# Neighbourhood attention on 64-row products: one query split for all heads in place of zero-padded buffers

## The chip, the cores and the metric

One Trainium2 chip, of which the kernel uses one core. The metric is the device time of one execution in microseconds (us); less is better. All engines of the core run side by side and wait for each other on semaphores.

## The reference

Two transformer blocks follow one another on 512 tokens of width 1024. The change lies in the second one (two layers, `l` = 0 and 1), in its neighbourhood attention. Each of 4 heads of width 64 has 512 queries; layer 0 also has 256 context queries, which attend to the context alone:

```python
s_loc = einsum('brqhd,brikhd->bhrqik', qg, k_band) * scale + bias   # 8 grid rows of 64 keys
s_loc = where(in_win, s_loc, -inf)
s_ctx = einsum('brqhd,blhd->bhrql', qg, k_ctx) * scale              # 256 context keys
p = softmax(concatenate([s_loc, s_ctx], -1))
o = einsum(p_loc, v_band) + einsum(p_ctx, v_ctx)
# context queries, layer 0 only
yc_b = dense_attention(q_ctx, k_ctx, v_ctx)
```

Everything is float32. The contraction of a score is over the 64 channels of one head.

## The kernel before

All work is written out by hand for each engine's queue, with semaphores between them; nothing is reordered by a scheduler. Most of the time goes to weight products ("units", function `gemm`): a float32 operand is split into a high part, rounded to the TensorE's fp32r format, and a low part (the rest), and `product` (lines 592 to 595) makes three matmuls: hi by hi, lo by hi, hi by lo. L593, L594 and L595 are the lines of all such matmuls, of the units and of the scores of neighbourhood attention alike.

After the projections of a layer come two attentions, one after the other: differential attention ("diff", lines 1633 for its exponentials and 2296 to 2307 for maximum and mix) and neighbourhood attention ("na"). Both go through `attention`, which works on items: one head and one tile of 128 queries. Layer 0 has 24 items (16 of 768 keys, then 8 context items of 256 keys), layer 1 has 16. For item i TensorE does, in this order:

1. the scores of item i + 2 (`na_score`), into one of two PSUM areas, once the exponential of item i has been taken;
2. the value products of item i - 1 (L989), once ScalarE has copied its transposed probabilities (`pt`, L1623);
3. the transposes of the probabilities of item i (L1001).

VectorE adds the bias (L2359), takes the maximum (L2362), scales a finished head (L2321), and in between squares the diff output (L2335, L2337). ScalarE takes the exponential (L1663) and makes the copy L1623. At item 6 both split the first unit of the output projection (ScalarE L1209, VectorE L1820).

Two heads share the 128 partitions of a query or key tile: head h has rows 64 (h % 2) to 64 (h % 2) + 63 of chunk h // 2. The kernel before still contracts over all 128 rows. For that it keeps zero-padded queries, `qz_hi[parity]` and `qz_lo[parity]`: tiles whose other 64 rows are zero. VectorE clears the four of them before diff attention of each layer (L2340), and for each head in turn ScalarE fills the 64 rows of the high part (`nqz_his`, L1639) and VectorE those of the low part (`nqz_los`, L2375): the first head near the end of diff attention, the next three at the beginning of na, the context heads as their turn comes. The keys (`nak`, `nakc`) are split once, for all heads (ScalarE L1647, L1652; VectorE L2379, L2382).

```python
q_hi, q_lo = (z[it.head % 2][:, c, tok] for z in (qz_hi, qz_lo))
if not it.ctx:
    product(dst[:, 0:S], q_hi, q_lo, nak_hi[:, c, :], nak_lo[:, c, :], True, True)
a_ = 0 if it.ctx else S
product(dst[:, a_:a_ + SC], q_hi, q_lo, nakc_hi[:, c, :], nakc_lo[:, c, :], True, True).then_inc(na_s, 1)
```

Of the kernel before, what the change touches and what calls it, by code (L numbers as in the profile page):

```python
# [17 lines left out]
F32 = mybir.dt.float32  # L18
F32R = mybir.dt.float32r
ALU = mybir.AluOpType  # L20
# [3 lines left out]
P = 128  # L24
DM = 1024
KT = DM // P
S = 512
SC = 256
# [15 lines left out]
HD = 64  # L44
# [95 lines left out]
def build(nc, d, out):  # L140
# [16 lines left out]
    with ctx:  # L157
        def at(name, shape, dtype, offset):

            return nc.alloc_sbuf_tensor_at(name, shape, dtype, offset=offset)  # L160
# [44 lines left out]
        H0 = o  # L205
# [106 lines left out]

        qz_hi = [at(f"qz_hi{i}", [P, 2, S], F32R, H0 + 4096 * i) for i in range(2)]
        qz_lo = [at(f"qz_lo{i}", [P, 2, S], F32R, H0 + 8192 + 4096 * i) for i in range(2)]
        nak_hi = at("nak_hi", [P, 2, S], F32R, Q2 + 8192)
        nakc_hi = at("nakc_hi", [P, 2, SC], F32R, Q2 + 20480)
# [25 lines left out]
        def result_bank(par, j):  # L342
# [49 lines left out]
        (df_s, df_split, df_mx, df_e1, df_e2, df_comb, df_t, df_pt, df_pv, df_out, ss_ready, ystd_ready, yd_ready, df_hi,  # L392
         nqz_ready, qz_zero, nqzhi_done, nk_hi, nk_split) = (
            sem(n_) for n_ in ("df_s1", "df_split", "df_max", "df_e1", "df_e2", "df_comb", "df_t", "df_pt", "df_pv", "df_out",
                               "df_squares", "df_std", "df_normed", "df_hi", "nqz_ready", "qz_zero",
                               "nqz_hi_done", "nk_hi", "nk_split"))
        na_s, na_mx, na_exp, na_t, na_pt, na_pv, na_out = (
# [193 lines left out]
        def _(pe):  # L591
            def product(dst, lhi, llo, rhi, rlo, start, stop):
                pe.matmul(dst, lhi, rhi, start=start, stop=False)  # L593
                pe.matmul(dst, llo, rhi, start=False, stop=False)  # L594
                return pe.matmul(dst, lhi, rlo, start=False, stop=stop)  # L595
# [408 lines left out]
            for l in range(2):  # L1004
# [119 lines left out]
                def na_score(i, it):  # L1124
                    c = it.head // 2
                    tok = slice(it.tile * P, (it.tile + 1) * P)
                    dst = S3[i % 2]
                    if it.pos == 0:
                        pe.wait_ge(nqz_ready, g0 + it.group + 1)
                    if i < 2:  # L1130
                        pe.wait_ge(df_e2, i0 + len(its) - 1 + i)
                    else:
                        pe.wait_ge(na_exp, i0 + i - 1)
                    q_hi, q_lo = (z[it.head % 2][:, c, tok] for z in (qz_hi, qz_lo))
                    if not it.ctx:
                        product(dst[:, 0:S], q_hi, q_lo, nak_hi[:, c, :], nak_lo[:, c, :], True, True)
                    a_ = 0 if it.ctx else S
                    product(dst[:, a_:a_ + SC], q_hi, q_lo, nakc_hi[:, c, :], nakc_lo[:, c, :], True, True).then_inc(na_s, 1)

# [59 lines left out]
        def _(act):  # L1199
# [364 lines left out]
            for l in range(2):  # L1564
# [71 lines left out]

                def nqz_his(it):
                    r_ = slice(HD * (it.head % 2), HD * (it.head % 2 + 1))
                    act.copy(qz_hi[it.head % 2][r_, it.head // 2, 0:SC if it.ctx else S],  # L1639
                             (naqc if it.ctx else naq)[r_, it.head // 2, :]).then_inc(nqzhi_done, 1)  # L1640

                df_exps(0, its[0])
                for i in range(N_):
                    if i + 1 < N_:
                        df_exps(i + 1, its[i + 1])
                    if i == N_ - 4:
                        act.copy(nak_hi[:], nak[:]).then_inc(nk_hi, 1)  # L1647
                    elif i == N_ - 3:
                        act.wait_ge(qz_zero, 4 * (l + 1))
                        nqz_his(first_of[0])  # L1650
                    elif i == N_ - 2:
                        act.copy(nakc_hi[:], nakc[:]).then_inc(nk_hi, 1)  # L1652
                    take_pt(i, its[i], df_t, df_pt, df_pv)
                for it in first_of[1:4]:
                    nqz_his(it)

                def na_exps(i, it):
# [9 lines left out]
                for i in range(N_):  # L1667
                    if i + 1 < N_:
                        na_exps(i + 1, its[i + 1])
                    if its[i].pos == its[i].size - 1 and its[i].group + 4 < len(first_of):  # L1670

                        nqz_his(first_of[its[i].group + 4])
                    take_pt(i, its[i], na_t, na_pt, na_pv)
                    if i == 6:
                        hi(n + 9)
# [42 lines left out]
        def _(dve):  # L1718
# [487 lines left out]
            for l in range(2):  # L2206
# [131 lines left out]

                for z in (*qz_hi, *qz_lo):
                    dve.memset(z[:].bitcast(F32), 0.0).then_inc(qz_zero, 1)  # L2340
                df_max(0, its[0])
# [27 lines left out]

                def nqz_los(it):  # L2370

                    dve.wait_ge(nqzhi_done, g0 + it.group + 1)
                    r_ = slice(HD * (it.head % 2), HD * (it.head % 2 + 1))
                    w_ = SC if it.ctx else S
                    dve.tensor_tensor(qz_lo[it.head % 2][r_, it.head // 2, 0:w_], (naqc if it.ctx else naq)[r_, it.head // 2, :],  # L2375
                                      qz_hi[it.head % 2][r_, it.head // 2, 0:w_].bitcast(F32), ALU.subtract).then_inc(nqz_ready, 1)

                dve.wait_ge(nk_hi, 2 * l + 1)
                dve.tensor_tensor(nak_lo[:], nak[:], nak_hi[:].bitcast(F32), ALU.subtract).then_inc(nk_split, 1)  # L2379
                nqz_los(first_of[0])  # L2380
                dve.wait_ge(nk_hi, 2 * l + 2)
# [7 lines left out]
                for i in range(N_):  # L2389
                    if i < 3:  # L2390
                        nqz_los(first_of[i + 1])
                    if 3 <= i < 3 + len(first_of):
                        last = df_squares(first_of[i - 3])
                        if i - 3 == len(first_of) - 1:
                            last.then_inc(ss_ready, 1)
                            dve.tensor_tensor(yv, yv, bc(subln[:], 4 * T), ALU.mult)
                    if i and its[i - 1].pos == its[i - 1].size - 1:
                        na_take(its[i - 1])
                    if i + 2 < N_:

                        if its[i + 2].pos == 0 and not its[i + 2].ctx:
                            mask_bias(its[i + 2].head)
                        dve.wait_ge(na_exp, i0 + i + 1)
                        na_max(i + 2, its[i + 2])
                    if its[i].pos == its[i].size - 1 and its[i].group + 4 < len(first_of):
                        nqz_los(first_of[its[i].group + 4])
                    if i == 6:
                        lo(n + 9, (n + 9) % 2)
# [179 lines left out]
```

## Time and profile before

| | |
|---|---|
| runs shown | 3055.95, 3068.29, 3068.49 us, median 3068.29 |
| profiled execution | 3062.02 us, its span 3060.4 us |
| TensorE busy | 2931.8 us (96%), weight loads 2503.1 us (82%) |
| VectorE, ScalarE busy | 1688.0 us (55%), 988.0 us (32%) |
| na attention | 1605.7 to about 1680 us (layer 0), 2574.4 to about 2632 us (layer 1) |

The span is the time between the first and the last instruction of the profiled execution; 1.6 us lie around it. PE is TensorE's matmul, PEld its weight load, which runs beside matmuls; DVE is VectorE, ACT ScalarE, SP the engine that issues most DMAs. A row of the trace names the line, the engine, the operation and its tiles. "[0.53 <-X]" at its end says for how long the engine had been idle before it and what ended that.

### The profile page before, as it was taken

To read this page: it belongs to the slowest core of one execution; us is meant where nothing else is said; L and a number is where in the kernel's file an instruction comes from. 1 tells how busy PE (TensorE), PEld (TensorE's weight loads), DVE (VectorE), ACT (ScalarE), POOL (GpSimd) and SP (SyncE) were. 2 spreads that over 40 slices of the span, in tenths; PEclk is the share of its full clock that TensorE was granted. 3 is DMA by queue.
4 is the path that set the end of the run, shared out by engine and by line. 5 is a ranking of instruction groups with operands and counts; after the bars stand their busy time and mean duration, and the time that the engine had idled before them with its cause. 6 is when DMAs were issued, how large, how long until landed. Compare 5 with 4: busy or idle time off the path is not lost.

```text
span 3060.4 us, 39832 instructions
## 1 busy us (share of the span) xinstructions
PE 2931.8 (96%) x15873; PEld 2503.1 (82%) x15873; DVE 1688.0 (55%) x2280; ACT 988.0 (32%) x1367; POOL 106.5 (3%) x150
## 2 busy tenths in 40 slices
PE   6999999999999999999888999999999988899999
PEld 5888787979788888789777888888888967788887
DVE  5656655454556676464486555455555248554444
ACT  3333333232333222322265232122223226433222
POOL 0000000000001100000000000000000000000000
PEclk8999999999999999999979999999999999999999
DMA  6333344535234544233430213223322142122332
GB/s 236 115 123 114 113 152 139 173 111 164 73 117 124 180 147 131 97 100 97 110 84 15 83 35 96 85 84 91 101 76 83 56 114 53 56 74 86 103 105 73
DMA packets 269999, 319.00 MB, mean 104 GB/s; under 512 B 25323, under 2 KB 236667, under 8 KB 269852
## 3 DMA queue, kind: packets, MB, share of 16 engines
q1 hardware_dynamic: 243676, 232.83, 24.8%
q0 software_dynamic: 19456, 72.00, 7.7%
q10 hardware_dynamic: 6720, 12.06, 1.2%
q8 instruction: 110, 1.80, 0.3%
q14 instruction: 37, 0.30, 0.0%
HBM read 294.05 MB, written 11.27 MB: 100 GB/s over the span
## 4 chain that ended last, share of the span: by engine, by line
PE 83%; DVE 6%; ACT 3%; DVEq 2%; SPq 2%; issue 1%; DMA 1%; ACTq 0%
PE psum L593 24%; PE psum L594 24%; PE psum L595 24%; PE psum L989 2%; SPq L549 2%; PE psum L759 1%; PE psum L805 1%; PE psum L1001 1%; DVE n_t L1808 1%; DVE w_lo L1820 1%; DVE dneg L2296 1%; DMA ada<-in_w_ada 1%; PE psum L873 1%; DVEq L1807 1%; DVE sba L2307 1%
## 5 line engine op out<-in xcount | busy, mean ns | idle before, releaser
L1820 DVE TENSOR_TENSOR w_lo<-raw,w_hi 128x2048 fp32r<-128x2048 f32 (+1 forms) x244 | 435.3, 1784 | 421.7 <-ACT w_hi L1209 311.5
L593 PE MATMUL psum<-hs_hi,w_hi 128*128 128x512 f32 x1632 | 648.8, 398 | 14.8 <-DVE hs_lo L1812 5.7
L595 PE MATMUL psum<-hs_lo,w_hi 128*128 128x512 f32 x1632 | 638.8, 391 | 0.0
L594 PE MATMUL psum<-hs_hi,w_lo 128*128 128x512 f32 x1632 | 638.7, 391 | 0.0
L593 PEld LDWEIGHTS psum<-hs_hi,w_hi 128*128 128x128 f32 x1632 | 308.2, 189 | 89.5 <-issue 13.3
L595 PEld LDWEIGHTS psum<-hs_lo,w_hi 128*128 128x128 f32 x1632 | 308.2, 189 | 65.7
L594 PEld LDWEIGHTS psum<-hs_hi,w_lo 128*128 128x128 f32 x1632 | 308.7, 189 | 62.7 <-issue 1.2
L1874 DVE SCALAR_TENSOR_TENSOR ada_acc<-ada_raw,csil,ada_acc 128x512 f32<-128x512 f32 x392 | 279.7, 749 | 45.1 <-DMA ada_raw<-in_w_ada 25.7
L593 PE MATMUL psum<-mid_hi,w_hi 128*128 128x512 f32 x768 | 300.5, 391 | 0.0
L594 PE MATMUL psum<-mid_hi,w_lo 128*128 128x512 f32 x768 | 299.7, 390 | 0.0
L595 PE MATMUL psum<-mid_lo,w_hi 128*128 128x512 f32 x768 | 299.3, 390 | 0.0
L1217 ACT CAST w_hi<-raw 128x2048 fp32r<-128x2048 f32 (+1 forms) x138 | 191.4, 1387 | 325.6 <-PE psum L595 293.3
L2128 DVE SCALAR_TENSOR_TENSOR r_t<-psum,r_t 128x512 f32<-128x512 f32 x112 | 77.0, 690 | 327.8 <-ACT r_t L1508 327.6
L1209 ACT CAST w_hi<-raw 128x2048 fp32r<-128x2048 f32 (+1 forms) x106 | 174.5, 1646 | 216.1 <-PE psum L595 194.2
L2080 DVE SCALAR_TENSOR_TENSOR X<-psum,mod,X 128x512 f32<-128x512 f32 x216 | 158.1, 748 | 146.0 <-PE psum L595 145.8
L1508 ACT ACTIVATE r_t<-psum 128x512 f32<-128x512 f32 x112 | 66.9, 598 | 461.3 <-PE psum L595 461.2
L593 PE MATMUL psum<-w_hi,hs_hi 128*128 128x256 f32 x704 | 199.6, 284 | 0.0
L595 PE MATMUL psum<-w_lo,hs_hi 128*128 128x256 f32 x704 | 199.2, 283 | 0.0
L594 PE MATMUL psum<-w_hi,hs_lo 128*128 128x256 f32 x704 | 199.2, 283 | 0.0
L595 PEld LDWEIGHTS psum<-mid_lo,w_hi 128*128 128x128 f32 x768 | 144.5, 188 | 30.4
L593 PEld LDWEIGHTS psum<-mid_hi,w_hi 128*128 128x128 f32 x768 | 144.7, 188 | 29.1
L594 PEld LDWEIGHTS psum<-mid_hi,w_lo 128*128 128x128 f32 x768 | 144.7, 188 | 28.8
(354 smaller groups left out, 4610.7 us busy)
## 6 DMA issues: line engine op xcount, KB each, us to landing
raw<-in_w_in SPq DMA_DIRECT2D x56, 1024.0 KB, 5.2
ada_raw<-in_ada_w POOLq DMA_DIRECT2D x96, 512.0 KB, 4.3
raw<-in_w_ff SPq DMA_DIRECT2D x48, 1024.0 KB, 5.5
raw<-in_w_ff SPq DMA_DIRECT2D x96, 512.0 KB, 3.4
ada_raw<-in_w_ada POOLq DMA_DIRECT2D x32, 512.0 KB, 4.8
raw<-in_w_in SPq DMA_DIRECT2D x24, 512.0 KB, 4.7
ada<-in_w_ada SPq DMA_DIRECT2D x4, 2048.0 KB, 18.8
raw<-in_w_ret_out SPq DMA_DIRECT2D x16, 512.0 KB, 3.4
```

Source lines behind the costliest of these rows:

```text
L549: sp.dma_start(dst[32 * q:32 * q + 32, t0:8:4, c0:c0 + w].bitcast(F32), src[r0:r0 + 32].bitcast(F32)).then_inc(landed, 16)
L593: pe.matmul(dst, lhi, rhi, start=start, stop=False)
L594: pe.matmul(dst, llo, rhi, start=False, stop=False)
L595: return pe.matmul(dst, lhi, rlo, start=False, stop=stop)
L989: mm = pe.matmul(O2[:, it.pos * HD:(it.pos + 1) * HD], pt2[:, t, :], values[:, t + 6 - nt, it.head * HD:(it.head + 1) * HD], start=t == 0, ...
L1209: act.copy(w_hi[n % 2][:, 0:kt], raw[n % 2][:, 0:kt]).then_inc(hi_done, 1)
L1217: act.copy(w_hi[n0_ % 2][:, 0:kt], raw[n0_ % 2][:, 0:kt]).then_inc(hi_done, 1)
L1508: act.activation(r_t[r_][:], result_bank((p0 + j) % 2, r_)[:], ACT.Relu).then_inc(relu_done, 1)
L1820: dve.tensor_tensor(w_lo[par][:, 0:kt], raw[par][:, 0:kt], w_hi[par][:, 0:kt].bitcast(F32), ALU.subtract).then_inc(lo_done, 1)
L1874: last = dve.scalar_tensor_tensor(out=acc[:, v, :], in0=ada_raw[par][:, kk, :], scalar=c_, in1=acc[:, v, :], op0=ALU.mult, op1=ALU.add)
L2080: last = dve.scalar_tensor_tensor(out=X[:, q, :], in0=G[2 * par + r_][:], scalar=gates[0][:, q:q + 1], in1=X[:, q, :], op0=ALU.mult, op1=A ...
L2128: dve.scalar_tensor_tensor(out=r_t[r_][:], in0=bank_, scalar=0.0, in1=r_t[r_][:], op0=ALU.max, op1=ALU.mult).then_inc(psum_free, 1)
```

## The change

The queries are split once for all four heads, and the score products take only the 64 rows of the head, of queries and keys alike. The zero-padded tiles, their memsets and the eight (layer 0) or four (layer 1) pairs of copies by head are gone.

```diff
-        qz_hi = [at(f"qz_hi{i}", [P, 2, S], F32R, H0 + 4096 * i) for i in range(2)]
-        qz_lo = [at(f"qz_lo{i}", [P, 2, S], F32R, H0 + 8192 + 4096 * i) for i in range(2)]
+        naq_hi = at("naq_hi", [P, 2, S], F32R, H0)
+        naq_lo = at("naq_lo", [P, 2, S], F32R, H0 + 4096)
+        naqc_hi = at("naqc_hi", [P, 2, SC], F32R, H0 + 8192)
+        naqc_lo = at("naqc_lo", [P, 2, SC], F32R, H0 + 10240)
...
# TensorE, na_score
-                    if it.pos == 0:
-                        pe.wait_ge(nqz_ready, g0 + it.group + 1)
+                    if it.pos == 0 and it.head == 0:
+                        pe.wait_ge(nq_split, 2 * l + (2 if it.ctx else 1))
...
-                    q_hi, q_lo = (z[it.head % 2][:, c, tok] for z in (qz_hi, qz_lo))
+                    rows = slice(HD * (it.head % 2), HD * (it.head % 2 + 1))
+                    q_hi, q_lo = (z[rows, c, tok] for z in ((naqc_hi, naqc_lo) if it.ctx else (naq_hi, naq_lo)))
                     if not it.ctx:
-                        product(dst[:, 0:S], q_hi, q_lo, nak_hi[:, c, :], nak_lo[:, c, :], True, True)
+                        product(dst[:, 0:S], q_hi, q_lo, nak_hi[rows, c, :], nak_lo[rows, c, :], True, True)
                     a_ = 0 if it.ctx else S
-                    product(dst[:, a_:a_ + SC], q_hi, q_lo, nakc_hi[:, c, :], nakc_lo[:, c, :], True, True).then_inc(na_s, 1)
+                    product(dst[:, a_:a_ + SC], q_hi, q_lo, nakc_hi[rows, c, :], nakc_lo[rows, c, :], True, True).then_inc(na_s, 1)
...
# ScalarE, in the loop over the items of diff attention
                     elif i == N_ - 3:
-                        act.wait_ge(qz_zero, 4 * (l + 1))
-                        nqz_his(first_of[0])
+                        act.copy(naq_hi[:], naq[:]).then_inc(nqhi_done, 1)
                     elif i == N_ - 2:
                         act.copy(nakc_hi[:], nakc[:]).then_inc(nk_hi, 1)
+                        if wc:
+                            act.copy(naqc_hi[:], naqc[:]).then_inc(nqhi_done, 1)
...
-                for it in first_of[1:4]:
-                    nqz_his(it)
...
-                    if its[i].pos == its[i].size - 1 and its[i].group + 4 < len(first_of):
-                        nqz_his(first_of[its[i].group + 4])
...
# VectorE
-                for z in (*qz_hi, *qz_lo):
-                    dve.memset(z[:].bitcast(F32), 0.0).then_inc(qz_zero, 1)
...
-                nqz_los(first_of[0])
+                dve.wait_ge(nqhi_done, 2 * l + 1)
+                dve.tensor_tensor(naq_lo[:], naq[:], naq_hi[:].bitcast(F32), ALU.subtract).then_inc(nq_split, 1)
...
-                    if i < 3:
-                        nqz_los(first_of[i + 1])
+                    if i == 0 and wc:
+                        dve.wait_ge(nqhi_done, 2)
+                        dve.tensor_tensor(naqc_lo[:], naqc[:], naqc_hi[:].bitcast(F32), ALU.subtract).then_inc(nq_split, 1)
...
-                    if its[i].pos == its[i].size - 1 and its[i].group + 4 < len(first_of):
-                        nqz_los(first_of[its[i].group + 4])
```

TensorE has the same instructions in the same order, 9189 rows before and after, with other operands. (`wc` is true in layer 0.)

ScalarE at the end of diff attention of layer 0, from the exponentials of the last but one item on. Before:

```order
L1633 ACTIVATE sba_211,dden<-psum,dneg 128x256
L1633 ACTIVATE sbb_200,dden<-psum,dneg 128x256
L1639 CAST qz_hi_203<-naq 64x512
L1623 COPY pt_213<-psum 128x256
L1633 ACTIVATE sba_212,dden<-psum,dneg 128x256
L1633 ACTIVATE sbb_201,dden<-psum,dneg 128x256
L1652 CAST nakc_hi<-nakc 128x512
L1623 COPY pt_213<-psum 128x256 x2
L1639 CAST qz_hi_204<-naq 64x512
L1639 CAST qz_hi_203<-naq 64x512
```

After:

```order
L1636 ACTIVATE sba_211,dden<-psum,dneg 128x256
L1636 ACTIVATE sbb_200,dden<-psum,dneg 128x256
L1647 CAST naq_hi<-naq 128x1024
L1626 COPY pt_213<-psum 128x256
L1636 ACTIVATE sba_212,dden<-psum,dneg 128x256
L1636 ACTIVATE sbb_201,dden<-psum,dneg 128x256
L1649 CAST nakc_hi<-nakc 128x512
L1651 CAST naqc_hi<-naqc 128x512
L1626 COPY pt_213<-psum 128x256 x2
L1659 ACTIVATE sba_211,den<-psum,stat_81 128x768
```

The 64x512 cast became one of 128x1024, and a 128x512 one stands new ahead of the last two copies of diff attention; the casts behind these copies are gone. In layer 1 the same holds without the `naqc` cast.

VectorE from there to the third maximum of na. Before:

```order
L2379 TENSOR_TENSOR nak_lo<-nak,nak_hi 128x1024
L2375 TENSOR_TENSOR qz_lo_205<-naq,qz_hi_203 64x512
L2382 TENSOR_TENSOR nakc_lo<-nakc,nakc_hi 128x512
L2351 TENSOR_TENSOR na_bias<-na_bias,na_mask 128x896
L2318 RECIPROCAL rden<-dden 128x2
L2321 TENSOR_TENSOR y_diff<-psum,rden 128x2x64
L2359 TENSOR_TENSOR psum<-psum,na_bias 128x512
L2362 TENSOR_REDUCE stat_81<-psum 128x1
L2359 TENSOR_TENSOR psum<-psum,na_bias 128x512
L2362 TENSOR_REDUCE stat_81<-psum 128x1
L2375 TENSOR_TENSOR qz_lo_206<-naq,qz_hi_204 64x512
```

After:

```order
L2362 TENSOR_TENSOR nak_lo<-nak,nak_hi 128x1024
L2364 TENSOR_TENSOR naq_lo<-naq,naq_hi 128x1024
L2366 TENSOR_TENSOR nakc_lo<-nakc,nakc_hi 128x512
L2342 TENSOR_TENSOR na_bias<-na_bias,na_mask 128x896
L2311 RECIPROCAL rden<-dden 128x2
L2314 TENSOR_TENSOR y_diff<-psum,rden 128x2x64
L2350 TENSOR_TENSOR psum<-psum,na_bias 128x512
L2353 TENSOR_REDUCE stat_81<-psum 128x1
L2350 TENSOR_TENSOR psum<-psum,na_bias 128x512
L2353 TENSOR_REDUCE stat_81<-psum 128x1
L2376 TENSOR_TENSOR naqc_lo<-naqc,naqc_hi 128x512
```

The subtraction ahead of na's first scores covers 1024 columns of 128 rows in place of 512 of 64 rows; the later ones, by head, are gone but for one of the context queries.

## Rows read from the trace of the kernel before

**Rows 1.** Windows: stretch, busy us (count) of PE, PEld, DVE, ACT, POOL, clock, DMA

```profile
1614.00:1620.00 6.00, 6.00 (x49) 5.64 (x48) 5.65 (x9) 3.48 (x6) 0.00 (x0) 1.00 0.01 3
2578.00:2623.00 45.00, 42.95 (x324) 39.54 (x324) 36.62 (x52) 25.77 (x44) 0.00 (x0) 1.00 0.08 24
```

**Rows 2.** Chain that ended last, one na item: start, us, engine, tile, line

```profile
1612.83 0.23 PE psum L593
...
1613.53 0.12 PE psum L593
...
1613.89 1.39 PE psum L989 x12
1615.28 0.66 PE psum L1001 x6
```

**Rows 3.** Timeline, around the 33-row matmuls of a bias table: start, us, instruction

```profile
477.59 0.39 PE L595 MATMUL psum<-hs_lo,w_hi 128*128 128x512 f32 x1
477.91 0.29 PEld L830 LDWEIGHTS psum<-onehot,rel 33*128 33x128 f32 x2 [0.35 <-issue]
...
479.94 0.40 PEld L832 LDWEIGHTS psum<-onehot,rel 33*128 33x128 f32 x2
480.16 0.59 PE L832 MATMUL psum<-onehot,rel 33*128 33x256 f32 x2
480.68 0.19 PEld L593 LDWEIGHTS psum<-hs_hi,w_hi 128*128 128x128 f32 x1 [0.33 <-issue]
...
481.02 0.40 PE L594 MATMUL psum<-hs_hi,w_lo 128*128 128x512 f32 x1
```

**Rows 4.** Timeline, first weight load of a unit behind full-row float32 matmuls (L792)

```profile
419.82 0.19 PEld L593 LDWEIGHTS psum<-hs_hi,w_hi 128*128 128x128 f32 x1
```

**Rows 5.** Timeline, diff attention of layer 1: last memset, scores of the second head

```profile
2511.14 0.91 DVE L2340 MEMSET qz_lo<- 128x1024 f32 x1 [0.16 <-issue]
...
2524.64 0.98 PE L1105 MATMUL psum<-ks,qs 128*128 128x512 f32 x4 [2.73 <-DMA ks<-dfkc_lo]
```

**Rows 6.** Timeline, end of diff attention, layer 0 and (last row) layer 1

```profile
1597.46 1.05 ACT L1647 CAST nak_hi<-nak 128x1024 fp32r<-128x1024 f32 x1
...
1599.57 0.62 ACT L1639 CAST qz_hi<-naq 64x512 fp32r<-64x512 f32 x1
...
1600.41 0.37 ACT L1623 COPY pt<-psum 128x256 f32<-128x256 f32 x1 [0.23 <-PE psum L1001]
...
1602.42 0.37 ACT L1623 COPY pt<-psum 128x256 f32<-128x256 f32 x1 [0.21 <-PE psum L1001]
...
1603.18 1.22 DVE L2379 TENSOR_TENSOR nak_lo<-nak,nak_hi 128x1024 fp32r<-128x1024 f32 x1
...
2565.99 0.80 ACT L1623 COPY pt<-psum 128x768 f32<-128x768 f32 x1
```

**Rows 7.** Timeline, PE ahead of value products with context scores beside the wait

```profile
1661.15 1.55 PE L989 MATMUL psum<-nav,pt 128*128 128x64 f32 x12 [0.54 <-ACT pt L1623]
```

**Rows 8.** Chain that ended last, context items of layer 0

```profile
1669.16 0.38 ACT pt L1623
```

**Rows 9.** Timeline, the stall behind the unit that is split at item 6, both layers

```profile
1639.02 0.42 DVE L2375 TENSOR_TENSOR qz_lo<-naqc,qz_hi 64x256 fp32r<-64x256 f32 x1
...
1640.87 0.41 PE L1001 MATMUL psum<-ident,sba 128*128 128x128 f32 x2 [2.21 <-DVE sgu L2321]
...
2606.84 0.41 PE L1001 MATMUL psum<-ident,sba 128*128 128x128 f32 x2 [0.70 <-DVE sgu L2321]
```

**Rows 10.** Windows, columns as in rows 1: behind a 33-row block; behind the stall

```profile
494.00:500.00 6.00, 6.00 (x21) 4.52 (x20) 3.03 (x4) 2.04 (x3) 0.00 (x0) 0.72 0.45 168
...
1642.00:1649.00 7.00, 7.00 (x33) 6.66 (x31) 6.25 (x10) 2.79 (x6) 0.00 (x0) 0.52 0.01 2
```

**Rows 11.** Chain that ended last, values and transposes of an item at the low clock

```profile
1642.32 2.62 PE psum L989 x12
1644.94 1.28 PE psum L1001 x6
```

More of the change, by code:

```diff
@@ L392, in build @@
         (df_s, df_split, df_mx, df_e1, df_e2, df_comb, df_t, df_pt, df_pv, df_out, ss_ready, ystd_ready, yd_ready, df_hi,
-         nqz_ready, qz_zero, nqzhi_done, nk_hi, nk_split) = (
+         nq_split, nqhi_done, nk_hi, nk_split) = (
             sem(n_) for n_ in ("df_s1", "df_split", "df_max", "df_e1", "df_e2", "df_comb", "df_t", "df_pt", "df_pv", "df_out",
-                               "df_squares", "df_std", "df_normed", "df_hi", "nqz_ready", "qz_zero",
-                               "nqz_hi_done", "nk_hi", "nk_split"))
+                               "df_squares", "df_std", "df_normed", "df_hi", "na_q_split", "na_q_hi",
+                               "nk_hi", "nk_split"))
         na_s, na_mx, na_exp, na_t, na_pt, na_pv, na_out = (
@@ L1635, in df_exps @@
                                        accum_out=dden[:, it.group % 2, half, it.pos:it.pos + 1]).then_inc(done, 1)
[L1637 to L1640, printed above, removed]
                 df_exps(0, its[0])
@@ L2368, in na_take @@
                          sgu[:, t0:t0 + it.size, GW + it.head * HD:GW + (it.head + 1) * HD], na_out)
[L2370 to L2376, printed above, removed]
                 dve.wait_ge(nk_hi, 2 * l + 1)
                 dve.tensor_tensor(nak_lo[:], nak[:], nak_hi[:].bitcast(F32), ALU.subtract).then_inc(nk_split, 1)
-                nqz_los(first_of[0])
+                dve.wait_ge(nqhi_done, 2 * l + 1)
+                dve.tensor_tensor(naq_lo[:], naq[:], naq_hi[:].bitcast(F32), ALU.subtract).then_inc(nq_split, 1)
                 dve.wait_ge(nk_hi, 2 * l + 2)
```

## Prediction

> **What bounds the kernel now.** I read three views in this order. The windows first: in the middle of na attention TensorE is busy all of 6.00 us, VectorE 5.65 and ScalarE 3.48, at the full clock of 2.4 GHz; layer 1 looks alike, 42.95 of 45.00 us [rows 1]. So here TensorE leads and VectorE is close behind. The chain of waits says the same more sharply: one item of 768 keys is nothing but TensorE, three score matmuls of 0.23 us, three of 0.12, value products 1.39 and transposes 0.66, together 3.10 us [rows 2]. Whatever lengthens an item on TensorE lengthens the kernel; whatever leaves ScalarE or VectorE inside an item saves nothing. The timeline last, for what a matmul on fewer rows does, and for the ends of the stage, where the order of waits differs.
>
> **What the change leaves alone.** A matmul's time here goes by its columns, and these stay: 512 and 256. Fewer rows do not shorten it: in a 33-row stretch the load of 479.94 starts together with the pass ahead of it, and its own matmul at 480.16, so a float32 pass of 256 columns takes 0.22 us [rows 3]; full-row float32 transposes take 0.11 us for 128 columns [rows 2], the same rate. The number of matmuls and loads is the same.
>
> **The main term: changing the row size.** The only matmuls on part of the rows so far are the bias tables. Ahead of them the last full-row matmul starts at 477.59 and, at 0.23 us, is through at 477.82; the load of the 33-row weights begins only at 477.91, idle 0.35 us, and its matmul can't stream before that load of some 0.10 us is in, so at 478.01: 0.19 us lost. On the way back the last pass is through at 480.16 + 0.43 = 480.59, the full-row load begins at 480.68 after 0.33 us of idleness, and the first product streams at 481.02 - 0.23 = 480.79: 0.20 us lost [rows 3]. The four bias tables show the same both ways. Behind full-row float32 matmuls the load of the next unit shows no idle time at all [rows 4]: the loss comes with the row size, not with the data type. In the new kernel every score block stands between full-row transposes and full-row value products, so it pays 0.20 us twice.
>
> Blocks on the chain, in each layer: scores 0, 1 and 2 follow one another and pay one pair. Scores 3 to 15 make 13 blocks, of which two (9 and 10) lie in the stall behind the split of the next unit, where TensorE idles 2.21 us in layer 0 and 0.70 us in layer 1 [rows 9]. In layer 0 their four changes, 0.80 us, fit; in layer 1 they are spread over this idleness and an earlier one ahead of scores 10, so I count them as hidden too. That leaves 12 pairs a layer, 24 in all: 48 x 0.20 = **+9.6 us**. Bounds: nothing, if 64 rows do not change the size as 33 do, and 28 pairs at 0.25 us a change, +14. I take 0.20, the nearest row.
>
> Context items, layer 0: scores 16 to 18 run while TensorE awaits the copy of the probabilities, with 0.54 us still idle [rows 7], so 0.40 more fits. Scores 19 to 23 have only the copy of 0.38 us as cover [rows 8]; a context block is three matmuls of 0.12, 0.35 us, and becomes 0.75: 0.33 us over cover and gap, five times, **+1.7 us** (bounds 0 and 2).
>
> **The splits.** Near the end of diff attention ScalarE stands in the chain. The cast for item N - 3 grows from 0.62 to the 1.05 us of a 128x1024 cast [rows 6]. In layer 1 the copy behind it starts without a wait, so +0.44. In layer 0 the copy had 0.23 us of idleness before it, so 0.2 shows; then the new 128x512 cast, taken at the 0.62 of 512 columns, stands ahead of a copy with 0.21 of idleness: +0.4 more. Together **+1.1 us** (bounds 0.5 and 1.6). VectorE's subtraction grows from 512 to 1024 columns, 1.22 us [rows 6]; this is hidden in layer 1, where the value products of the last diff item are still running, and in layer 0 by the delay of ScalarE just counted. If that cover is gone it costs half of the 1.22, 0.6.
>
> Removed: four memsets a layer, 0.91 us each, and the later copies by head. The memsets are over or nearly so when the first maxima are due; what they hold up in layer 1, at most one memset, is absorbed by the second head, whose scores wait 2.73 us for the DMA of stacked keys [rows 5]. That DMA does not depend on them: nothing. The subtractions in items 0 to 2 sit on VectorE, which was not the bound and gets 0.4 us more room per item: nothing. One subtraction, 0.42 us, stands in layer 0's stall, ahead of the VectorE step that releases TensorE [rows 9]: **-0.4 us**. ScalarE's casts behind the last diff copy had no one waiting. New waits: TensorE's on the split queries comes twice in place of eight times and is met where the keys' is met; behind VectorE's wait at item 0 stands the third maximum, but the cast it awaits was done before.
>
> **Sum.** 9.6 + 1.7 + 1.1 - 0.4 = **+12.0 us** on the profiled execution's 3062.0 (span 3060.4), 3074.0. The median of the runs shown, 3068.3, lies 6.3 above that execution, which would give 3080.3. The runs themselves scatter by 12.5 us, so I take the middle, **3077**.
>
> **The clock, both signs.** It is at its lower level (1.2 GHz) for most of 1642 to 1649 in layer 0, granted 0.52, right behind TensorE's 2.21 us of idleness: 7 x 0.48 = 3.4 us lost [rows 9, 10]. With switches inside the stall and 0.4 us less of it, about 1.0 us of idleness stays, and layer 1 kept its clock with 0.70 [rows 9]. So up to -3.4. Against it stands the next rival; in the forecast I let the two cancel.
>
> **The rivals.**
> - *Half the rows count as less work, and the clock falls.* From 494 to 500 TensorE is busy without a gap and yet granted only 0.72: this is right behind the third of the four 33-row blocks, 1.7 us lost [rows 10]. The other three had no fall, and the full-row float32 stretches of like length had none. The scores are 1.05 of 3.5 us of an item, on 64 rows, with the rest full. Priced low: 29 us of such matmuls are ten bias blocks, a fall behind every fourth, each 1.7 to 3.4 us: 4 to 9. Priced high: at the low clock values and transposes take 3.90 us in place of 2.05 [rows 2, 11] and scores 1.05 more, 2.9 an item; every second of 28 items: 41. I take 22 in between: 3077 + 22 = **3099**, slower by over 0.5%. It decides once about two items stay at the low clock beyond the forecast. Chance 0.20.
> - *The row size costs nothing* (64 rows of fp32r are not treated as 33 of float32). Left are 1.1 - 0.4 = +0.7, and the fall in layer 0 stays or goes: 3062 + 3 to the middle of the runs = **3066**, down to 3062. Chance 0.12.
> - *Loads no longer run beside matmuls within a block.* Each of five loads of 0.10 us in a block would be bare: 28 x 5 x 0.10 = 14 more, **3091**. Against it: the load of 479.94 begins 0.2 us ahead of its matmul, while the one before streams, in the same 33 rows [rows 3]. Chance 0.03. The Trainium skill ("TensorE: Matmul & The Clock Gate", Part 3, The mechanism) says that a weight load overlaps running matmuls only where the row groups differ. By that rule this rival would hold; the row just named, and every full-row pair, disagree, so I give it no more.
>
> The same skill ("TensorEngine Tiling (Array Packing)", Theoretical Speedup) promises up to twice the speed where the contraction is 64 or less. By it the scores would shrink by half, some 15 us in all. It needs two tiles at work at once, and here all six matmuls of a block use the same 64 rows; the 33-row products above show no gain. I count it within the 0.02 below.
>
> **How the numbers follow.** Forecast 0.65 (9 to 16 us slower), clock 0.20, no cost 0.12, bare loads 0.03. A measurement of this kernel can tell about 0.5%, 15.3 us, from no change. Slower by more than that: a quarter of the forecast, 0.16, nearly all of the clock case, 0.19, and the bare loads, 0.03: 0.38. Faster by more: no sum reaches it, 0.02. The rest, 0.60, is within. The range goes from the no-cost case, 3061, to a little over the clock case, 3106; the forecast's own is 3068 to 3086.
>
> **What would show it.** Right: in na the score loads carry some 0.3 us of idleness behind transposes, value products likewise behind scores, an item takes 3.5 us, VectorE's share falls, and the number of matmuls is unchanged. The last diff copies come 0.4 to 0.6 us later. Wrong: items of 3.1 us (no size change), items of over 4 us at the full clock (bare loads), or a granted clock under 0.9 over the stage of layer 1, which is 1.00 now [rows 1]. Items shorter than 3.1 us would mean that VectorE, and not TensorE, had been the bound.

## The result and the profile after

The changed kernel takes 3150.9 us (median of four runs, 3147.7 to 3154.5); the kernel before, timed beside it on the same chip, 3066.0. The ratio is 1.028, with a 95% interval of 1.027 to 1.030: slower by some 85 us. Forecast were 3077, in a range up to 3106. The prediction was wrong, in size by far and in its range. Ratios here are estimated from the single runs and can differ from the quotient of two medians, by 0.4% at most. One execution, the longest on 72 rows, counts as slow and is left out of its ratio.

The page of the profile after, parts 1 and 2:

```profile
span 3146.0 us, 39797 instructions
PE 3028.6 (96%) x15873; PEld 2579.8 (82%) x15873; DVE 1677.2 (53%) x2263; ACT 983.2 (31%) x1358; POOL 106.5 (3%) x150
PEclk8999999999999999999865999999999986699999
```

TensorE has 96% of the span as before and the same number of matmuls, but nearly 97 us more to do. The last row says why: na attention lies in slices 21 and 22 (1573 to 1730 us) for layer 0 and in 34 and 35 (2595 to 2753 us) for layer 1, and there the row has 6, 5 and 6, 6: a granted clock of 0.5 to 0.7. The mean over the span is 0.942, where it was 0.974.

The stage can be timed from its first score matmul to the transposes that follow it (TensorE's timeline, before and then after, layers 0 and 1):

```profile
1605.73 0.77 PE L593 MATMUL psum<-nak_hi,qz_hi 128*128 128x512 f32 x1
1683.25 3.59 PE L1163 MATMUL psum<-ident,sgu 128*128 128x128 f32 x16 [3.58 <-DVE sgu L2321]
2574.40 0.48 PE L593 MATMUL psum<-nak_hi,qz_hi 128*128 128x512 f32 x1
2634.10 3.68 PE L1163 MATMUL psum<-ident,sgu 128*128 128x128 f32 x16 [2.25 <-DVE sgu L2321]
```

```profile
1603.26 0.79 PE L595 MATMUL psum<-nak_hi,naq_hi 64*128 64x512 f32 x1
1728.22 3.30 PE L1166 MATMUL psum<-ident,sgu 128*128 128x128 f32 x16 [3.12 <-DVE sgu L2314]
2616.34 0.50 PE L595 MATMUL psum<-nak_hi,naq_hi 64*128 64x512 f32 x1
2719.46 3.67 PE L1166 MATMUL psum<-ident,sgu 128*128 128x128 f32 x16 [1.32 <-DVE sgu L2314]
```

Layer 0's stage grew from 77.5 to 125.0 us, layer 1's from 59.7 to 103.1: +47.4 and +43.4, 90.8 together. All the rest of the program is 5.3 us shorter (2.5 ahead of layer 0's stage, 3.0 between the stages, 0.2 longer behind); the first experiment's profile, with the same splits, begins the stage at 1605.81, as before, so I give the 2.5 no cause.

Windows of the profile after; the first is a stretch of [rows 1], the next three the beginning of layer 1's stage, the last two most of each stage:

```profile
1614.00:1620.00 6.00, 6.00 (x25) 5.15 (x25) 2.65 (x3) 1.58 (x3) 0.00 (x0) 0.50 0.00 0
2617.00:2620.00 3.00, 1.71 (x11) 1.30 (x9) 2.23 (x3) 0.54 (x1) 0.00 (x0) 1.00 0.00 0
2620.00:2623.00 3.00, 2.49 (x12) 2.04 (x12) 1.99 (x4) 1.45 (x4) 0.00 (x0) 0.81 0.00 0
2623.00:2626.00 3.00, 3.00 (x11) 2.33 (x10) 1.11 (x2) 1.69 (x3) 0.00 (x0) 0.50 0.00 0
1653.00:1722.00 69.00, 68.08 (x269) 57.39 (x268) 23.24 (x45) 20.30 (x48) 0.00 (x0) 0.50 0.05 16
2634.00:2687.00 53.00, 53.00 (x204) 45.37 (x204) 22.05 (x31) 16.80 (x27) 0.00 (x0) 0.50 0.06 21
```

In six microseconds TensorE gets through 25 matmuls where it did 49, and is busy in all six both times. The clock is at its lower level (1.2 GHz) from 1594 to 1731 and from 2622 to 2724. Before, it fell at 1591 too, and was back at 1608; in layer 1 it did not fall before 2632, when the last scores (2621) were long done. From 1609 to 1719 and from 2622 to 2704 TensorE has not one idle stretch over 0.15 us, and the clock does not come back.

One item of the chain, TensorE's timeline at the lower level:

```profile
1624.56 0.79 PE L595 MATMUL psum<-nak_hi,naq_hi 64*128 64x512 f32 x1
1625.16 0.62 PE L596 MATMUL psum<-nak_hi,naq_lo 64*128 64x512 f32 x1
...
1626.44 0.41 PE L597 MATMUL psum<-nakc_lo,naq_hi 64*128 64x256 f32 x1
1626.78 2.82 PE L991 MATMUL psum<-nav,pt 128*128 128x64 f32 x12
1629.39 1.49 PE L1003 MATMUL psum<-ident,sba 128*128 128x128 f32 x6
1630.81 0.79 PE L595 MATMUL psum<-nak_hi,naq_hi 64*128 64x512 f32 x1
```

From one L595 to the next are 6.25 us, where the chain of [rows 2] takes 3.10. With VectorE and ScalarE at half their former share, their waits are gone: the stall of [rows 9] has none of its 2.21 us of idleness left.

The score loads and ScalarE's new casts (timelines of layer 1's stage and of the end of layer 0's diff attention):

```profile
2620.84 0.39 PE L596 MATMUL psum<-nak_hi,naq_lo 64*128 64x512 f32 x1
2620.85 0.18 PEld L597 LDWEIGHTS psum<-nak_lo,naq_hi 64*128 64x128 f32 x1
2621.07 0.39 PE L597 MATMUL psum<-nak_lo,naq_hi 64*128 64x512 f32 x1
...
2623.16 0.28 PEld L595 LDWEIGHTS psum<-nak_hi,naq_hi 64*128 64x128 f32 x1 [0.33 <-issue]
```

```profile
1596.50 1.07 ACT L1647 CAST naq_hi<-naq 128x1024 fp32r<-128x1024 f32 x1
1597.44 0.41 ACT L1626 COPY pt<-psum 128x256 f32<-128x256 f32 x1
```

Inside a block the load of the next matmul runs beside the one before, as on full rows, and 512 columns take 0.23 us. A block's first load has 0.33 us of idleness ahead of it, as at the 33-row blocks [rows 3]. The casts fit as [rows 6] had them.

### The profile page after: what moved, and what is told of

It is laid out like the page before. It is cut to its first block, busy times and chain, and to the rows that moved or that the text cites. A ratio compares the mean times of both kernels' runs of the same rounds, so it can differ in the third digit from the quotient of the medians.

```text
span 3146.0 us, 39797 instructions
## 1 busy us (share of the span) xinstructions
PE 3028.6 (96%) x15873; PEld 2579.8 (82%) x15873; DVE 1677.2 (53%) x2263; ACT 983.2 (31%) x1358; POOL 106.5 (3%) x150
## 4 chain that ended last, share of the span: by engine, by line
PE 85%; DVE 6%; ACT 2%; DVEq 2%; SPq 2%; issue 1%; DMA 1%; ACTq 0%
PE psum L595 24%; PE psum L596 24%; PE psum L597 24%; PE psum L991 4%; SPq L551 2%; PE psum L1003 2%; PE psum L761 1%; PE psum L807 1%; DVE n_t L1801 1%; DVE dneg L2289 1%; DMA ada<-in_w_ada 1%; PE psum L875 1%; DVE sba L2300 1%; DVEq L1800 1%; PE psum L794 1%
## 5 line engine op out<-in xcount | busy, mean ns | idle before, releaser
L595 PE MATMUL psum<-hs_hi,w_hi 128*128 128x512 f32 x1632 | 648.4, 397 | 9.5 <-DVE hs_lo L1805 5.4
L595 PEld LDWEIGHTS psum<-hs_hi,w_hi 128*128 128x128 f32 x1632 | 308.1, 189 | 83.9 <-DVE hs_lo L1805 8.8
L595 PE MATMUL psum<-mid_hi,w_hi 128*128 128x512 f32 x768 | 301.1, 392 | 0.0
L595 PE MATMUL psum<-w_hi,hs_hi 128*128 128x256 f32 x704 | 199.6, 284 | 0.0
L595 PEld LDWEIGHTS psum<-mid_hi,w_hi 128*128 128x128 f32 x768 | 145.1, 189 | 29.4
```

## The experiments

Two theories stand against each other at first: the time goes to the clock, because of what is computed on 64 rows; or to something else of the change (splits, waits, the changes of row size), with the clock as a follower.

**Everything of the change but the 64 rows.**

```diff
-                    rows = slice(HD * (it.head % 2), HD * (it.head % 2 + 1))
+                    rows = slice(0, P)
```

> The new kernel, but the score products run over all 128 rows of the same queries and keys (the two heads of a chunk are mixed, so the scores are others). Everything else of the change stays: splits, waits, no zero-padded tiles. If the 85 us come from the 64-row matmuls, by the clock or by the changes of row size, it takes 3065 to 3070 us, an item 3.1 us, the granted clock in na of layer 1 is 1.00. If they come from the splits or their waits, it stays near 3150.

Measured: 3060.1 us, ratio 0.998 (0.997 to 0.9995), 5 us under the range I gave. Windows of its profile, the stretches of [rows 1]:

```profile
1614.00:1620.00 6.00, 6.00 (x49) 5.69 (x48) 5.17 (x8) 3.41 (x7) 0.00 (x0) 1.00 0.01 3
2578.00:2623.00 45.00, 42.59 (x325) 39.13 (x323) 33.68 (x47) 26.08 (x44) 0.00 (x0) 1.00 0.07 24
```

The one-off splits, the casts and the new waits cost the kernel nothing. The whole loss lies in that one slice. The kernel before keeps its clock although half of the rows of its queries hold zeros, and this one has data in all of them: between these two it makes no difference to the clock whether the other 64 rows do something useful, as long as the matmuls span them.

The terms of the splits do show inside the trace. In layer 1 TensorE's wait ahead of the third last value products of diff attention grew from 0.89 to 1.20 us, and the wait behind the split at item 6 of layer 0 shrank from the 2.21 of [rows 9] to 1.85:

```profile
2565.45 1.55 PE L991 MATMUL psum<-dfv,pt 128*128 128x64 f32 x12 [1.20 <-ACT pt L1626]
1640.48 0.41 PE L1003 MATMUL psum<-ident,sba 128*128 128x128 f32 x2 [1.85 <-DVE sgu L2314]
```

**The changes of row size alone,** in the kernel before: one matmul of 8 columns on 64 rows ahead of each block, overwritten by it.

```diff
+                    pe.matmul(dst[:, 0:8], qz_hi[it.head % 2][0:HD, c, tok], (nakc_hi if it.ctx else nak_hi)[0:HD, c, 0:8], start=True, stop=True)
```

> The kernel before, with one 64-row matmul of 8 columns ahead of each score block (40 of them, overwritten by the block): two changes of row size per block, and next to no 64-row work. If the changes themselves, or the idleness they bring, make the clock fall, it is granted 0.5 in na and the time is near 3150. If the clock answers to the share of rows at work, it stays at 1.00 in layer 1, an item takes 3.10 + 0.40 + some 0.03 us, and the kernel is 10 to 14 us slower than before, 3076 to 3080: the price of the changes alone.

Measured: 3076.7 us, ratio 1.003 (1.002 to 1.005), mean clock 0.970. TensorE's timeline at the full clock:

```profile
1621.55 0.49 PE L593 MATMUL psum<-nak_hi,qz_hi 128*128 128x512 f32 x1
...
1624.74 0.27 PE L1135 MATMUL psum<-nak_hi,qz_hi 64*128 64x8 f32 x1
1624.94 0.49 PE L593 MATMUL psum<-nak_hi,qz_hi 128*128 128x512 f32 x1
```

An item takes 3.39 us in place of 3.10: 0.14 or 0.15 a change, the added matmul of 8 columns included. The forecast's main mechanism is real, at 11 us in all at most, and that is an eighth of the result. In its profiled execution the two stages are 4.2 and 4.4 us longer than before, and the clock also falls in layer 1, 0.8 us behind the first scores (2587.25), where it did not before; it is back after 3.4 us (2588.0 to 2591.4):

```profile
2588.00:2591.00 3.00, 3.00 (x10) 2.34 (x9) 1.59 (x2) 0.00 (x0) 0.00 (x0) 0.50 0.00 0
```

**72 rows, and then 96, for every head.** On 72 rows (`rows = slice(0, 72)`; the scores mix in rows of the other head):

> The new kernel with score products over rows 0 to 71 for every head (other scores): nearly as few rows as 64. If the row size changes only between up to 64 rows and more, there are no changes of size here. If the clock answers to the rows at work, it still falls, and the time is 3120 to 3145, an item at the low clock 5.8 to 6.1 us without idleness ahead of its loads. If it answers to the changes, or to the array being set to half its rows, the clock stays and the time is 3065 to 3070.

Measured: 3136.0 us (3094 to 3144), ratio 1.019 (1.011 to 1.026). The profiled execution is the longest of the four; three of them have a mean clock of 0.939 to 0.943, the shortest 0.957. No load has the 0.3 us of idleness ahead of it any more, and an item at the lower level takes 5.65 us (1624.73 to 1630.38 in its timeline), 0.60 less than on 64 rows. So 72 rows pay no change of size; yet:

```profile
1626.00:1651.00 25.00, 25.00 (x109) 23.71 (x109) 12.18 (x21) 6.86 (x12) 0.00 (x0) 0.50 0.00 1
2631.00:2681.00 50.00, 50.00 (x214) 47.13 (x214) 24.10 (x34) 17.32 (x28) 0.00 (x0) 0.50 0.06 22
```

These windows of its profile have the clock at 0.50 and TensorE busy throughout. So the theory that it is the size changes that hold the clock down is refuted. On 96 rows (`rows = slice(0, 96)`):

> Score products over rows 0 to 95 for every head (other scores). No change of size expected, as with 72 rows. If each row counts, the share stands between that of 72 rows (low for most of na) and of 128 (no low stretch of its own): fewer falls, 3060 to 3100. If only the full array counts as work, it is as with 72 rows, near 3136.

Measured: 3068.1 us, ratio 1.002 (1.001 to 1.003). The clock falls right behind the first blocks of layer 1 (at 2582.8), where the kernel before stays up, and is back after 3.4 us. Between 72 and 96 rows, out of 128, lies nearly the whole loss.

**A part of the products on 64 rows.** Only those with the 256 context keys, a third of the columns:

```diff
-                        product(dst[:, 0:S], q_hi, q_lo, nak_hi[rows, c, :], nak_lo[rows, c, :], True, True)
+                        product(dst[:, 0:S], naq_hi[:, c, tok], naq_lo[:, c, tok], nak_hi[:, c, :], nak_lo[:, c, :], True, True)
```

> The new kernel with only the products against the 256 context keys on 64 rows, those against the 512 keys on all rows (mixed heads, other scores): as many changes of row size as in the new kernel, a third of the 64-row work (half rows for 0.35 us of an item in place of 1.05). If the changes make the clock fall, near 3150. If the rows do, the fall is rarer or gone: between 3076 and 3110. If it is gone, 3076 to 3080.

Measured: 3070.9 us (3066 to 3087), ratio 1.003 (1.001 to 1.005), below my range for a clock that falls by the rows. Yet the profiled execution (3085.2, one of the longer ones) has the clock low for 31 and 17 us in layer 0 and for 17 in layer 1, and each time it comes back within the stage. And the other two thirds, those with 512 keys, on 64 rows with the context keys on all:

> The new kernel with the products against the 512 keys on 64 rows and those against the 256 context keys on all rows: 64-row work is 0.70 of the 1.05 us, all changes of size as before. If the clock answers to the 64-row work, it lies between the third (3071) and the whole (3151): I expect 3090 to 3140. If there is a single point at which it tips, it is at one of the two ends.

Measured: 3144.0 us, ratio 1.027 (1.025 to 1.029), clock at its lower level for 116 us in one piece in layer 0 and for 109 in layer 1. My range ended at 3140. With 0, 1, 2 and 3 thirds the times are 3060, 3071, 3144 and 3151, and the first step is no more than what the size changes cost by themselves (11 us): neither in rows nor in columns does the loss grow evenly, it tips.

**More work on full rows, the result left as it is.**

```diff
+                    for _ in range(2):
+                        if it.ctx:
+                            pe.matmul(dst[:, 0:SC], naqc_hi[:, c, tok], nakc_hi[:, c, :], start=True, stop=True)
+                        else:
+                            pe.matmul(dst[:, 0:S], naq_hi[:, c, tok], nak_hi[:, c, :], start=True, stop=True)
```

> The new kernel, all its products as they are, with more work: ahead of each score block two matmuls over all 128 rows, 512 columns (256 for a context item), overwritten by the block. If the clock answers to the share of rows at work, this raises the share and the clock may come back: an item then takes 3.50 + 2 x 0.23 = 4.0 us in place of 6.25, and the kernel some 3090 us, faster than the new one although it does more. If the clock does not come back, an item takes 6.25 + 0.86 and the time is near 3175.

Measured: 3103.6 us, ratio 1.013 (1.010 to 1.016): 80 added matmuls make the changed kernel 47 us faster. In its profile layer 1's stage has no fall at all; in layer 0 the clock is still low for 58 us (from 1594, ahead of the stage, on) and for 38. **The same two matmuls on the head's 64 rows** (`q_hi` and `nak_hi[rows, c, :]` in the lines above):

> The changed kernel with the same two added matmuls ahead of each score block as in the run with more full-row work (512 columns, 256 for context items), only that these too work on the head's 64 rows. Output unchanged. It asks what made that kernel 47 us faster than the changed one: that the added work used all rows, or only that TensorE had more to do. If work on 64 rows holds the clock down (my theory), nothing is won: 3151 plus 32 items x 0.43 us at the full clock, or x 0.86 at the lower one, 3165 to 3180, and the lower clock all through na attention of both layers. If more work of any kind keeps the clock up (rival): about 3104, as with full rows, and na attention of layer 1 at the full clock.

Measured: 3187.5 us, ratio 1.040 (1.038 to 1.041), a little over my bound: the added matmuls run at the lower level in all blocks but the first three of layer 1, and 29 x 0.86 + 3 x 0.43 + 8 x 0.43 is some 30 of the 37 us. Windows in layer 1's stage, of the full-row kernel and then of this one:

```profile
2622.00:2642.00 20.00, 19.35 (x123) 15.48 (x124) 12.34 (x19) 9.09 (x17) 0.00 (x0) 1.00 0.00 1
```

```profile
2660.00:2700.00 40.00, 40.00 (x146) 33.80 (x145) 15.52 (x23) 12.06 (x19) 0.00 (x0) 0.50 0.00 0
```

Same columns, same count, 84 us apart. It isn't that TensorE had too little to do; it had too little to do on all rows.

**Two tiles at work at once.** The products with 512 keys on the head's 64 rows and those with the context keys on the other 64, issued in turn into different banks, so that all 128 rows are in use while both run (the context scores are then another head's):

```diff
+                            mm1 = pe.matmul(dst[:, 0:S], l1, r1[rows, c, :], start=k_ == 0, stop=k_ == 2)
+                            mm2 = pe.matmul(dst[:, S:S + SC], l2, r2[other, c, :], start=k_ == 0, stop=k_ == 2)
```

> The new kernel with the two products of a block in turn, the 512 keys on the head's 64 rows and the 256 context keys on the other 64 (other scores against the context), in two PSUM banks. If matmuls on different halves of the array run side by side, the block shrinks from 1.05 to some 0.70 us, both halves are at work for part of it, and the clock may hold: an item of 3.1 to 3.2 us and 3065 to 3075. If they run side by side and the clock still falls, about 3130. If they do not, near 3151 or slower, with more idleness ahead of the loads.

Measured: 3091.9 us (3084 to 3127), ratio 1.013 (1.006 to 1.020), between my two cases. Its timeline in layer 1, at the lower level:

```profile
2597.47 0.79 PE L1145 MATMUL psum<-nak_hi,naq_hi 64*128 64x512 f32 x1 [2.16 <-ACT sba L1665]
2597.47 0.58 PE L1146 MATMUL psum<-nakc_hi,naq_hi 64*128 64x256 f32 x1
```

The two start together. The Trainium skill ("TensorEngine Tiling (Array Packing)", Theoretical Speedup) promises up to twice the speed for this; the rows agree that the tiles overlap. An item at the lower level takes 5.61 us against 6.25, and the clock comes back after 85 us in layer 0 and 27 us in layer 1, against 137 and 102. It still loses to products on all rows.

**The gap.** In layer 1 the fall comes right behind 1.79 us in which TensorE waits for the first exponentials, a gap that the kernel before has too. Eight full-row matmuls ahead of block 1 fill it:

```diff
+                    for _ in range(8 if i == 1 else 0):
+                        pe.matmul(dst[:, 0:S], naq_hi[:, c, tok], nak_hi[:, c, :], start=True, stop=True)
```

> The changed kernel with eight added matmuls of 512 columns on all rows ahead of score block 1 of each layer; their result is overwritten by the block. TensorE then has work where it otherwise idles 1.8 us between blocks 1 and 2 of layer 1, the gap behind which the clock fell in the changed kernel. Output unchanged. If 64-row work by itself takes the clock down (my theory), the fall comes all the same, some microseconds later, and stays: 3145 to 3165. If the fall needs the gap, and 64-row work only keeps the clock from coming back (rival), layer 1 stays at 2.4 GHz: the 52 us that its 104 us at the lower level cost are saved and 2 x 1.9 are added at most, about 3100.

Measured: 3150.8 us, ratio 1.027 (1.026 to 1.029), as the changed kernel. The clock fell at 2634, 9 us behind the first block's start, where it fell 5.6 us behind it in the changed kernel. But the gap wasn't gone:

```profile
2632.27 0.50 PE L595 MATMUL psum<-nak_hi,naq_hi 64*128 64x512 f32 x1 [0.99 <-ACT sba L1661]
```

0.99 us of it is left, because VectorE and ScalarE start no earlier, and the fall is right behind that. So this run doesn't tell the two theories apart. The next one bears on both.

**One burst of full-row work,** sixteen matmuls ahead of block 5 of each layer (the same lines with `16 if i == 5`):

> The changed kernel with one burst of sixteen added matmuls of 512 columns on all rows ahead of score block 5 of each layer (3.7 us at the full clock, 7.4 at the lower), overwritten by the block. Output unchanged. It asks whether one burst of full-row work brings the clock back, and whether it then stays. If it comes back and stays: layer 1 saves some 40 us and layer 0 about as much, less 11 us of bursts: 3070 to 3100. If it comes back and falls again within a few items (what I expect, since the fall of layer 1 came within 5 us of its first 64-row blocks): 3135 to 3160, with a short stretch at 1.00 behind each burst. If a burst does nothing: 3166.

Measured: 3125.0 us (3114 to 3136), ratio 1.020 (1.017 to 1.023), between my two cases. Its timeline and windows:

```profile
2632.28 4.29 PE L1139 MATMUL psum<-nak_hi,naq_hi 128*128 128x512 f32 x16
2636.50 0.49 PE L595 MATMUL psum<-nak_hi,naq_hi 64*128 64x512 f32 x1
...
2639.88 0.50 PE L595 MATMUL psum<-nak_hi,naq_hi 64*128 64x512 f32 x1
```

```profile
2609.00:2612.00 3.00, 2.11 (x18) 1.81 (x17) 2.62 (x5) 0.80 (x1) 0.00 (x0) 1.00 0.01 5
2613.00:2616.00 3.00, 2.45 (x9) 1.85 (x8) 2.17 (x3) 0.67 (x1) 0.00 (x0) 0.50 0.00 0
1626.00:1651.00 25.00, 23.84 (x157) 19.91 (x155) 14.94 (x24) 10.93 (x18) 0.00 (x0) 1.00 0.07 18
1653.00:1722.00 69.00, 64.50 (x261) 54.92 (x260) 23.28 (x45) 23.22 (x53) 0.00 (x0) 0.51 0.00 1
2634.00:2687.00 53.00, 46.71 (x326) 39.69 (x325) 28.97 (x42) 24.54 (x41) 0.00 (x0) 1.00 0.06 21
```

In both layers the clock comes back about 1 us into the burst (burst from 1625.03, clock from 1626.1; 2632.28 and 2633.1), and in layer 1 it stays at 2.4 GHz to the end of the stage: 53 us of the very items on 64 rows that ran at 1.2 GHz in the changed kernel. I had expected it to fall again within a few items; that theory is refuted. In layer 0 it stays up for some 27 us, until the split at item 6 leaves TensorE idle:

```profile
1651.83 0.41 PE L1003 MATMUL psum<-ident,sba 128*128 128x128 f32 x2 [1.64 <-DVE sgu L2316]
```

Behind this the clock falls, and now stays down for 68 us. The kernel before falls at the same place, and is back after 7 us. So scores on 64 rows amid full-row work need not take down a clock that is up, and they keep it down once it has fallen. The profiled execution took 3114 us, the shortest of the four, and the median is 11 above: how long the clock stays up differs between runs.

The rival, that the fall needs the gap of 1.8 us, doesn't hold either. Here the clock is at 1.00 up to the first scores of layer 1 (2611.85) and falls at 2612.6, within the first block and ahead of the wait for the exponentials, which begins at 2615.45. With two thirds on 64 rows it is the same (first scores 2611.75, fall 2612.5). Next to the kernels above, a fall near the first scores of layer 1 is common: 3.4 us with one matmul of 8 columns on 64 rows a block or with 96 rows, 17 us with a third, 27 us with two tiles, and 99 to 113 us in the five kernels with 64 or 72 rows in two thirds of the score work or more and no full-row work to end it. What the rows decide is above all how long it lasts.

**Context fills moved out of the stall,** in the kernel before; the 0.2% of the first experiment made one hope for something there.

```diff
-                    if its[i].pos == its[i].size - 1 and its[i].group + 4 < len(first_of):
-                        nqz_los(first_of[its[i].group + 4])
+                    if its[i].pos == 1 and 3 < its[i].group + 3 < len(first_of):
+                        nqz_los(first_of[its[i].group + 3])
```

> The kernel before with full-row products, with one part of what the change does to the queries done in another way: the four fills of the context queries are moved from the last item of a head to the second item of the head after it, on ScalarE and on VectorE, so that none lies in the stall behind the unit that is split at item 6 of layer 0. The run with the one-off split and products over all rows was 0.9982 of the kernel before. If that gain came from the subtraction in the stall, this kernel shows part of it: about -0.4 us, and up to -4 us where the fall of the clock behind the stall goes too. If it came from the copies and memsets removed elsewhere, or is scatter: 1.000, within 0.1%. I expect 0.9995.

Measured: 3067.0 us, ratio 1.0007 (0.9997 to 1.0018): nothing. Its trace has the wait behind the split at 1.84 us in place of 2.21, near the 0.4 that I had priced, and that is too little to show in a run's time. The subtraction in the stall isn't where the first experiment's 0.2% came from; where it did stays open. No version here that computes the reference beat the kernel before.

## Why the prediction was wrong

- **What bounds the kernel, and what a matmul costs by its columns**: right. TensorE leads, 512 columns take 0.23 us on 64 rows too, loads and matmuls keep their number. The splits, priced at +1.1 us, cost 0.3 in layer 1 where I had 0.44 (a wait of 0.89 us became 1.20), and the stall lost the 0.4 us that I had given it (2.21 to 1.85). Neither shows in the time of the first experiment, which is 5.6 us below the kernel before.
- **"Changing the row size: 48 x 0.20 = +9.6 us"**: mechanism right, size a little high. At the full clock two changes cost 3.38 - 3.10 = 0.28 us an item, from the burst experiment's item (2636.50 to 2639.88), so 0.14 each; the row I took was at another shape, 33 rows of float32. At the lower level they cost 0.60 an item. With the context blocks I had 9.6 + 1.7 = 11.3 us; the kernel with nothing but such changes paid 11. That the totals agree so well is partly luck: each change is a third cheaper than I took it, and the 11 also hold 40 added matmuls and a fall of the clock of 3.4 us.
- **"In the forecast I let the two cancel"**, said of the clock: this step failed. It put the clock's loss at nothing, and that loss is where the 74 us between forecast and result went. The two stages are at the lower level for 222 us, before for 15; half of the difference, an estimate of 104 us, is what that costs, and some of it comes back as waits that vanish. The rival's price of an item was right: 2.9 us over the forecast's 3.5; measured are 6.25 - 3.38 = 2.87. What was wrong was the number of items. I took a fall for an episode, "a fall behind every fourth" block or "every second of 28 items", that each time ends by itself as those of [rows 10] do. But a fall ends through work, and I had not asked what work ended it in the rows before me: there it was always items on all rows. With the scores on 64 rows it ended only with the stage. By an estimate from these rows, some sixteen items in layer 0 and fourteen in layer 1, at 3.15 us over [rows 2]'s 3.10, are the 91 us, less the stalls that vanish beneath.
- The mark I had set, a granted clock under 0.9 in layer 1's stage, is what came: 0.50. It was the rival with a chance of 0.20, whose upper price of 41 us was half of what it cost.
- **Bare loads**: refuted, by the row at 2620.85 above. The Trainium skill ("TensorE: Matmul & The Clock Gate", Part 3, The mechanism) lists that loads overlap running matmuls only where the row groups differ, though the paragraph above that list also lets a load into a background weight buffer go ahead. The row at 2620.85, on the same 64 rows as the matmul beside it, disagrees with the list.
- **No cost**: refuted by the 0.33 us ahead of each block.

What is shown: the loss comes with the rows alone (first experiment), not through size changes (72 rows), and more full-row work lessens it while the same work on 64 rows adds to it. A burst of full-row work brings the clock back, and the same items then kept it for 53 us in one layer and 27 in the other. What is open: the rule by which rows count, and what starts the fall near the first scores of layer 1. It comes ahead of the gap or behind it, and with 8 columns on 64 rows too; only the kernels with nothing but full-row scores, and the one with two full-row matmuls ahead of each block, have none in their one profile each. Waits of 0.89 us at the end of diff attention lie ahead of it in all of them, and no run parts these from the scores.

## What to carry to other kernels

A matmul on half of the rows saves no time, and amid full-row work it can hold TensorE's clock at half speed for a hundred microseconds, where a fall ends within a few on full rows; zero-padding an operand to all 128 rows is then the faster form, even where it costs copies and memsets. When a trace shows a short fall of the clock that ends by itself, ask which work ended it and whether the change leaves that work as it is; price the case in which it doesn't end as the whole stage at the lower level. Where half rows can't be avoided, try two tiles at once, or a few microseconds of full-row matmuls behind a place where TensorE has idled: each gave back part of the loss here.

## What the hardware did that I had not expected

- TensorE was busy without a gap for 53 us (2634 to 2687 of the profile after) at a granted clock of 0.50. Being busy does not suffice to get 2.4 GHz back; with 64 rows in about 30% of an item's time it failed, with 96 rows there it took 3.4 us in layer 1.
- The same instructions run at either level, depending on what came before: items on 64 rows at 6.25 us in one kernel, at 3.38 in another, with nothing between the two but sixteen matmuls some items earlier.
- Adding 80 matmuls whose results are thrown away took 47 us off.
- 72 rows show no change of size, 64 do: idleness of 0.33 us ahead of the first load of a block at 64 rows and none at 72.
